# A two-layer block on one core: the down projections computed as seven products of halves instead of eight

## The reference

```python
D_FF = 2816; DEEPNORM_ALPHA = (2 * DEPTH) ** 0.25
def conv_ffn(x, w_up, conv_w, conv_b, w_down):
    up = x @ w_up                                  # 512 x 1024 by 1024 x 5632
    a, g = up[..., :D_FF], up[..., D_FF:]
    g = causal_dwconv(g, conv_w) + conv_b
    return (jax.nn.gelu(g) * a) @ w_down           # 512 x 2816 by 2816 x 1024
# in the layer:
x = layer_norm(alpha * x + conv_ffn(x, ...), ln_ffn_g[layer], ln_ffn_b[layer])
```

## Time and profile before

| | before |
|---|---|
| median of three runs | 1784.28 us |
| profiled execution, its own time | 1786.04 us |
| its span | 1784.2 us |
| PE busy | 1758.9 us (99% of the span) |
| DVE, ACT, POOL busy | 1027.2, 652.2, 99.5 us |
| granted TensorE clock | 0.998 mean |
| DMA | 189.67 MB, 106 GB/s |

### The profile page before, as it was taken

One profiled execution on the slowest core, in us unless ns is written; L12 is line 12 of the kernel. 1 busy time (PEld: TensorE's weight loads), 2 busy tenths in 40 slices (PEclk: granted clock), 3 DMA queues, 4 the chain that ended last, 5 costly groups with the idle time before them and its releaser, 6 DMA issues.

```text
span 1784.2 us, 27491 instructions
## 1 busy us (share of the span) xinstructions
PE 1758.9 (99%) x11571; PEld 1472.9 (83%) x11571; DVE 1027.2 (58%) x1480; ACT 652.2 (37%) x1013; POOL 99.5 (6%) x136
## 2 busy tenths in 40 slices
PE   8999999999999999999999999999999999999998
PEld 7888988988888889888998888888888767777766
DVE  5567267444445555454726755566556585566784
ACT  5232352323324333213235232232343553344552
POOL 3102002000000001000200200000001000011000
PEclk9999999999999999999999999999999999999999
DMA  9323312433333324333331264444431422112512
GB/s 302 111 94 113 113 49 77 147 95 102 98 95 107 94 83 128 109 95 117 108 107 60 89 195 153 142 154 130 138 94 36 151 60 73 38 38 63 176 36 83
DMA packets 146010, 189.67 MB, mean 106 GB/s; under 512 B 7800, under 2 KB 95092, under 8 KB 145120
## 3 DMA queue, kind: packets, MB, share of 16 engines
q1 hardware_dynamic: 140928, 172.59, 31.2%
q0 software_dynamic: 3488, 10.07, 1.8%
q10 hardware_dynamic: 1472, 5.26, 0.8%
HBM read 181.58 MB, written 6.30 MB: 105 GB/s over the span
## 4 chain that ended last, share of the span: by engine, by line
PE 93%; DVE 4%; issue 1%; ACT 1%; POOL 1%; DMA 0%; SPq 0%; DVEq 0%; ACTq 0%
PE ps L329 28%; PE ps L331 27%; PE ps L330 27%; PE ps L970 2%; PE ps L518 1%; PE ps L2222 1%; PE ps L2242 1%; PE ps L1628 1%; PE ps L2236 1%; PE ps L2256 0%; DVE LATE L2303 0%; PE ps L2359 0%; PE ps L982 0%; DVE WL L313 0%; PE ps L1652 0%
## 5 line engine op out<-in xcount | busy, mean ns | idle before, releaser
L313 DVE TENSOR_TENSOR WL<-RAW,WH 128x1024 fp32r<-128x1024 f32 x289 | 350.8, 1223 | 501.3 <-ACT WH L303 500.0
L329 PE MATMUL ps<-XH,WH 128*128 128x512 f32 (+1 forms) x1416 | 524.6, 371 | 3.4 <-DVE XL L1498 1.6
L303 ACT ACTIVATE WH<-RAW 128x1024 fp32r<-128x1024 f32 x289 | 303.5, 1058 | 597.5 <-PE ps L331 570.0
L331 PE MATMUL ps<-XH,WL 128*128 128x512 f32 (+1 forms) x1416 | 518.2, 366 | 0.0
L330 PE MATMUL ps<-XL,WH 128*128 128x512 f32 (+1 forms) x1416 | 517.9, 366 | 0.0
L329 PE MATMUL ps<-WH,XH 128*128 128x512 f32 x784 | 312.7, 399 | 2.4 <-DVE WL L313 1.1
L329 PEld LDWEIGHTS ps<-XH,WH 128*128 128x128 f32 x1416 | 267.5, 189 | 51.4 <-issue 6.1
L331 PE MATMUL ps<-WH,XL 128*128 128x512 f32 x784 | 305.8, 390 | 0.0
L330 PE MATMUL ps<-WL,XH 128*128 128x512 f32 x784 | 305.5, 390 | 0.0
L331 PEld LDWEIGHTS ps<-XH,WL 128*128 128x128 f32 x1416 | 267.4, 189 | 43.4
L330 PEld LDWEIGHTS ps<-XL,WH 128*128 128x128 f32 x1416 | 267.7, 189 | 40.9
(11 more groups left out here) (359 smaller groups left out, 1797.5 us busy)
## 6 DMA issues: line engine op xcount, KB each, us to landing
RAW<-ffn_w_up SPq DMA_DIRECT2D x176, 256.0 KB, 3.2
RAW<-ffn_w_down SPq DMA_DIRECT2D x44, 512.0 KB, 3.7
RAW<-w_in SPq DMA_DIRECT2D x33, 512.0 KB, 3.9
RAW<-xa_wkv SPq DMA_DIRECT2D x32, 512.0 KB, 3.8
RAW<-c_w_in SPq DMA_DIRECT2D x24, 512.0 KB, 3.8
LATE<-w_ada SPq DMA_DIRECT2D x24, 512.0 KB, 4.8
RAW<-xa_wq SPq DMA_DIRECT2D x16, 512.0 KB, 5.7
RAW<-xa_wo SPq DMA_DIRECT2D x16, 512.0 KB, 3.7
```

What stands on the lines that cost most here:

```text
L303: e.activation(halves_of(i)[0][:, :, 0:w], raw(i)[:, :, 0:w], ACT.Copy).then_inc(*w_hi.up(i))
L313: e.tensor_tensor(wl[:, :, 0:w], raw(i)[:, :, 0:w], wh[:, :, 0:w].bitcast(F), ALU.subtract).then_inc(*w_lo.up(i))
L329: e.matmul(o, lh, rh, start=start, stop=False)
L331: return e.matmul(o, ll, rh, start=False, stop=stop)
```

## The change

Both down projections are computed by Strassen's scheme in Winograd's form. The product is cut into halves: tokens 0 to 255 and 256 to 511, k rows 0 to 1407 and 1408 to 2815, output columns 0 to 511 and 512 to 1023. Seven products of halves take the place of eight. Each has 11 k tiles, two token tiles (u = 0, 1) and three matmuls of 512 columns: 66 matmuls. Their operands are sums:

- Weights: four sums t1 to t4 of quarter matrices (2.9 MB each) are made in memory by DMAs that POOL issues, a plain copy from memory to memory and then an accumulating one (`sums_pool`, six steps for each layer, spread over the stages before). Each copy and each accumulation is 2 DMAs, 16 DMAs for a layer. SP waits for them before it loads a chunk made of them.
- Tokens: four sums for each of 11 pairs of tiles of hT by four DVE operations of 256 columns (`token_sums`; nine times during the last five blocks of the up projection, twice in the down projection). One stays in hT, three go to memory (`token_out`) and two kinds come back (`token_in`) through a ring of three places, all issued by POOL.
- PE runs chunks of half the size of work: 40 chunks for a layer (22 that serve two products each, then 6 for each of the products c, d, e; the last of the 6 is half full), each used by 12 matmuls instead of 24. In the program of ACT and DVE a "step" s is one such chunk: at step s they split chunk s + 5 and the token items of `items_at(s)`.
- The results are combined by DVE in steps 20 to 29, then d closes rows 0 and 1 (steps 30 to 33), and e closes rows 2 and 3. In d and e the last four chunks are run for u = 0 first and then for u = 1.

```diff
+    def w_fast(l):
+
+        first["ffn", l] = len(chunks)
+        w = I["ffn_w_down"][l]
+        for name, k in FAST:
+            if name == "a":
+                chunks.append(([((0, 1), 512, w[128 * k:128 * k + 128, 0:512].unsqueeze(1)),
+                                ((1, 2), 512, d_sum[l][k][:, 2:3, :])], 512, ("t1", l, k)))
+            if name == "b":
+                chunks.append(([((0, 2), 512, d_sum[l][k][:, 0:2, :])], 512, ("t3", l, k)))
+            if name in "cd":
+                c = 512 * "cd".index(name)
+                chunks.append(([((0, pair(k)), 512, w[1408 + 256 * k:1408 + 256 * k + 128 * pair(k), c:c + 512].rearrange(
+                    "(k p) n -> p k n", p=P))], 512, None))
+            if name == "e":
+                v = d_sum[l][2 * k:2 * k + pair(k)]
+                chunks.append(([((0, pair(k)), 512, v[:, :, 3, :].rearrange("k p n -> p k n"))], 512, ("t4", l, 2 * k + pair(k) - 1)))
...
+            if chunks[i][2] is not None:
+                what, l, k = chunks[i][2]
+                for name in (("t2", "t3") if what == "t3" else (what,)):
+                    e.wait_ge(*sum_in[name][k // 6].at(l))
...
+    def token_sums(e, l, k):
+
+        pair_of, last = token_place(l)
...
+        e.wait_ge(*ffn_v.at(("h", l, 11 + k)))
+        e.tensor_tensor(s3, a11, a21, ALU.subtract).then_inc(*ffn_v.up())
+        e.wait_ge(*latest["V"])
+        e.tensor_tensor(a21, a21, a22, ALU.subtract).then_inc(*ffn_v.up(("s1", l, k)))
+        e.wait_ge(*latest["V"])
+        e.tensor_tensor(s2, a21, a11, ALU.subtract).then_inc(*ffn_v.up())
+        e.wait_ge(*latest["V"])
+        e.tensor_tensor(last, a12, s2, ALU.add).then_inc(*ffn_v.up(("s", l, k)))
...
+    def item_hi(e, l, n):
+
+        name, k = ITEMS[n]
+        if n < 2:
+            e.wait_ge(*(gemm.at(("kvv", 1, 3, 1)) if l else xa_pe.at(("pv", 0, 3, 1))))
+        elif name == "C":
+            for a in range(2 * k, 2 * k + pair(k)):
+                e.wait_ge(*x_lo.at(("item", l, ITEMS.index(("A", a)))))
+        elif RINGED.index(n) < 8:
+            e.wait_ge(*gemm.at((("up", l, 10), 3)))
+        else:
+            e.wait_ge(*gemm.at(("used", first["ffn", l] + item_last(RINGED[RINGED.index(n) - 8]))))
+        if name == "A":
+            e.wait_ge(*ffn_v.at(("s1", l, k)))
+        elif name in "BD":
+            i = LOADED.index((name, k))
+            e.wait_ge(*tok_in[i % 3].at((l, i)))
+        else:
+            e.wait_ge(*ffn_v.at(("h", l, 10 + 2 * k + pair(k))))
+        e.activation(item_view(n, item_home(l, n)[0]), item_from(n), ACT.Copy).then_inc(*x_hi.up(("item", l, n)))
+
+    def item_lo(e, l, n):
+
+        e.wait_ge(*x_hi.at(("item", l, n)))
+        hi, lo = item_home(l, n)
+        e.tensor_tensor(item_view(n, lo), item_from(n), item_view(n, hi).bitcast(F), ALU.subtract).then_inc(
...
+
+        def added(name, g, src):
+            e.wait_ge(*sum_in[name][g].at((l, "copy")))
+            e.dma_start(part(name, g), src, accum_op=ALU.add).then_inc(*sum_in[name][g].up(l))
+        for g in range(2):
+            if step == 0:
+                copied("t1", g, block(0, 1, g))
+                copied("t3", g, block(0, 1, g))
+            if step == 1:
+                added("t1", g, block(0, 0, g))
+                added("t3", g, block(1, 1, g))
+            if step == 2:
+                e.wait_ge(*sum_in["t3"][g].at(l))
+                copied("t2", g, part("t3", g))
+            if step == 3:
+                added("t2", g, block(0, 0, g))
+            if step == 4:
+                e.wait_ge(*sum_in["t2"][g].at(l))
+                copied("t4", g, part("t2", g))
+            if step == 5:
+                added("t4", g, block(1, 0, g))
...
+    def tokens_pool(e, l):
+        for k in range(9):
+            token_out(e, l, k)
+            if 2 < k < 6:
+                token_in(e, l, k - 3)
+
+    def down_pool(e, l):
+        for i in range(3, 17):
+            token_in(e, l, i)
+            if i == 6:
+                token_out(e, l, 9)
+            if i == 8:
+                token_out(e, l, 10)
...
+            e.wait_ge(*w_lo.at(i0 + s))
+            ready(s)
+            of = ((1, 0), (5, 256)) if name == "A" else ((6, 256), (7, 0))
+            for half, (p, at) in enumerate(of):
+                for u in range(2):
+                    key = ("down", l, p, u)
+                    if k == 0:
+                        ps.take(key)
+                        for w in ps.vacant(key):
+                            e.wait_ge(*w)
+                    r = product(key, s, at + 128 * u, i0 + s, half, k == 0, k == 10)
+                    names = [key] * (k == 10) + [("used", i0 + s)] * (half and u)
+                    if names:
+                        r.then_inc(*gemm.up(*names))
+            if k == 10:
+                ps.back(*[("down", l, p, u) for p, _ in of for u in range(2)])
+
+        def part(name, q, u):
+            i, m, key = i0 + FAST.index((name, q)), ITEMS.index((name.upper(), q)), ("down", l, {"c": 2, "d": 3, "e": 4}[name], u)
+            if u == 0:
+                e.wait_ge(*w_lo.at(i))
+                ready(m)
+            if q == 0:
+                ps.take(key)
+                for w in ps.vacant(key):
+                    e.wait_ge(*w)
+            for k in range(pair(q)):
+                at = 256 * u + 128 * k if name == "e" else 256 * k + 128 * u
+                r = product(key, m, at, i, k, (q, k) == (0, 0), q == 5)
+            names = [key] * (q == 5) + [("used", i)] * u
+            if names:
+                r.then_inc(*gemm.up(*names))
...
+                part("c", q, u)
+        ps.back(("down", l, 2, 0), ("down", l, 2, 1))
+        for name in "de":
+            for q in range(2):
+                for u in range(2):
+                    part(name, q, u)
+            for u in range(2):
+                for q in range(2, 6):
+                    part(name, q, u)
+                    if name == "e" and (u, q) in ((0, 5), (1, 3)):
+                        behind(u)
+        ps.back(*[("down", l, p, u) for p in (3, 4) for u in range(2)])
...
+    def items_at(s):
+
+        got = [s + 8] if s < 14 else []
+        got += [ITEMS.index(("C", q)) for q, at in enumerate((2, 6, 10, 13, 16, 18)) if at == s]
+        got += [ITEMS.index(("D", q)) for q, at in enumerate((14, 16, 17, 19, 22, 23)) if at == s]
+        return got + [ITEMS.index(("E", q)) for q, at in enumerate((24, 26, 28, 29, 30, 31)) if at == s]
...
+        def row(t):
+            u = t % 2
+            if t < 2:
+                e.wait_ge(*gemm.at(("down", l, 3, u)))
+                e.wait_ge(*ln_v.at((n, "x12", u)))
+                add(3, t, 1)
+                stats_of(t, 1)
+            else:
+                e.wait_ge(*gemm.at(("down", l, 4, u)))
+                e.wait_ge(*ln_v.at((n, "x21", u)))
+                add(4, t, 0)
+                stats_of(t, 0)
+            norm_g_dve(e, XR[:, t, :], n, t, 2, GB[:, 0:1024], gb_in.at(n))
...
+                if s == 20:
+                    e.wait_ge(*dn_a.at(("u", l, u)))
+                    scaled(u, 0, U[u]).then_inc(*ln_v.up((n, "x11", u)))
+                if s == 21:
+                    e.wait_ge(*gemm.at(("down", l, 6, u)))
+                    e.wait_ge(*ln_v.at((n, "x11", u)))
+                    e.tensor_tensor(U[u], U[u], ps.tile(("down", l, 6, u))[:, :], ALU.add).then_inc(
+                        *ps.empties(("down", l, 6, u), ln_v, (n, "sum", u)))
+                if s == 22:
+                    e.wait_ge(*ln_v.at((n, "sum", u)))
+                    e.wait_ge(*gemm.at(("down", l, 5, u)))
+                    e.tensor_tensor(Y[u], ps.tile(("down", l, 5, u))[:, :], U[u], ALU.subtract).then_inc(
+                        *ps.empties(("down", l, 5, u), ln_v, (n, "y", u)))
+                if s == 23:
+                    e.wait_ge(*ln_v.at((n, "y", u)))
+                    scaled(u, 1, Y[u]).then_inc(*ln_v.up((n, "x12", u)))
+                if s == 24:
+                    e.wait_ge(*gemm.at(("down", l, 7, u)))
+                    scaled(2 + u, 0, ps.tile(("down", l, 7, u))[:, :]).then_inc(*ln_v.up((n, "ax21", u)))
+                if s == 25:
+                    scaled(2 + u, 1, Y[u]).then_inc(*ln_v.up((n, "ax22", u)))
+                if s == 26:
+                    e.wait_ge(*ln_v.at((n, "ax22", u)))
+                    e.tensor_tensor(x(2 + u, 1), x(2 + u, 1), ps.tile(("down", l, 7, u))[:, :], ALU.subtract).then_inc(
+                        *ps.empties(("down", l, 7, u), ln_v, (n, "x22", u)))
+                if s == 27:
+                    e.wait_ge(*ln_v.at((n, "ax21", u)))
+                    e.tensor_tensor(x(2 + u, 0), x(2 + u, 0), U[u], ALU.add).then_inc(*ln_v.up((n, "x21", u)))
+                if s == 28:
+                    e.wait_ge(*gemm.at(("down", l, 2, u)))
+                    add(2, u, 0)
+                    stats_of(u, 0)
+                if s == 29:
+                    e.wait_ge(*ln_v.at((n, "x22", u)))
```

(32 more changed lines are left out.)

390 lines of the change are left out of this document (253 added, 137 removed).

## The result

| | before | after |
|---|---|---|
| median | 1784.13 us (4 runs, 1783.92 to 1784.6) | 1764.99 us (4 runs, 1762.02 to 1770.95) |
| ratio, 95% interval | | 0.9897 [0.9871, 0.9922] |
| profiled execution, its span | 1786.04, 1784.2 us | 1764.57, 1762.8 us |

The kernel is 1.0% faster. Forecast was 1760.3 us with a range of 1753.5 to 1774. The profiled execution came to 1764.57 where the sum said 1762.0.

What follows compares the result with a forecast made beforehand. PE, busy 99% of the span, was taken as the bound. Terms -29.9 -0.4 +4.8 +0.7 +0.8 = -24.0 us took the profiled 1786.0 to 1762.0, median 1760.3 us, range 1753.5 to 1774.

Steps and rivals of the forecast that it cites:

- PE's own work: Both down projections: 132 matmuls fewer at 0.2267 us each, 29.9 us off (about 28.5 by the skill's 518 cycles).
- Ordinary steps and the up projection's end: ACT and DVE keep up in ordinary down-projection steps, and token sums in the up projection's last five blocks cost nothing: 0.
- Start of the down projection: DVE's convolutions and item 7's token load at the down projection's start: 0 taken, bounds 0 and 3 us a layer.
- (c): Steps 20 to 33 of each down projection: PE waits for DVE's chunks 37 and 38, 2.4 us a layer, 4.8 in both.
- Chunk 42 behind the first layer: After the first layer's last down-projection matmul PE waits 0.7 us for this weight chunk from DVE; bounds 0 and 3.
- The second weight copy: End of the second layer: two weight copies instead of one between row 3's square and scaling, 0.8 us; bounds 0 and 1.1.
- The sums: Weight sums made in memory beside the weight loads: 0, bounds 0 and 3 us at each of four places.
- rival 3: Weight loads land late at the four bursts of weight sums, 1.5 to 3 us each: 1768 us; chance 0.12.
- the cover: Time by which weight loads may land late without a stall, read behind a norm as some 15 us.
- From the profiled execution to the median: Whole kernel: the median lies 1.76 us below the profiled execution, the same difference applied after the change.
- Rival 2: DVE bounds the down projections' last products: 8 us a layer instead of 2.4, 1.5 at the start; 1774.5 us; chance 0.17.

Runs made afterwards that it cites:

- the experiment: The changed kernel with one weight copy instead of two between row 3's square and its scaling, end of the second layer: 1764.07 us, ratio 0.9875.
- the late work: The changed kernel with six more statistics readings on DVE (4.1 us a layer) in steps 22 to 27 of each down projection: 1773.88 us, ratio 0.9933.

## Why the prediction held, and where it did not

- *PE's own work*, -29.9: right. 132 instructions fewer, 0.226 us apart. The spacing decides for 29.9 and against 28.5 (518 cycles); that PE's busy time fell by 28.7 does not speak for the latter, as other things changed in it too.
- *Ordinary steps and the up projection's end*, 0: right. No wait of PE between 560 and 640 us. DMA was put at 240 GB/s and is 240 and 253; DVE's busy share was put at 85% and is 89%.
- *Start of the down projection*, 0: right, no wait there.
- *(c), 2.4 us a layer*: right in the first layer (2.54) and in its place: two waits, for chunks 37 and 38, 1.3 and 1.1 forecast, 1.08 and 1.46 measured. In the second layer it is **mis-sized by 1.8 us** (4.24). The step that failed took both layers as alike. It followed DVE's queue, but not POOL's, in which `rms_pool(0)` stood before `norm_pool(1)`: the prediction said only that the norms stand behind the token DMAs. Of the 1.8 us, POOL's order is 0.9, and 0.6 is the chunk of down weights that landed late in the first profile; 0.3 stay open.
- *Chunk 42 behind the first layer*, 0.7: did not appear, as the waits in product e had already delayed PE. With these removed it came, at 1.2 us.
- *The second weight copy*, 0.8: in its place it is 0.9 us (from square to scaling 2.09 us before, 2.96 after). Of this 0.2 is left at the next stage's first product (12.44 us before, 12.61 after, from the bias product on), and 0.3 to 0.5 in the experiment. The 0.2 flatters it: in the trace of before the clock fell at 1387.1 us, and the transposes of row 3 began 0.9 us after their scaling had ended (1388.24 to 1389.15), behind slow ones; after, they began at once.
- *The sums*, 0: nearly right for the time, wrong in the landing (14.4 us where 7.5 was the most allowed; by turns between the queues rival 3 reckoned with twice a load's usual time, and it was four times, which decides). Rival 3 had the mechanism, at a much smaller price than its 8 us: 1.3 us in the first profile (0.55 near 380 us, 0.8 at the attention's start), 0.2 to 4.0 in others. The prediction read the cover only behind a norm. In the up projection it took the lead of five chunks as enough for DVE's token sums and did not ask whether the loads beside the sums of weights would use it up, as they did from 340 to 375 us.
- *From the profiled execution to the median*: I took off 1.76 us, since before's profile lay so much above its median. After's profile lies 0.4 us below its median. Of the 4.7 us between 1760.3 and 1764.99, 2.2 are this step, and 2.6 the sum: +1.8 and +0.1 in (c), +1.3 for the sums, -0.7 for chunk 42 and -0.6 for the copy make 1.9. Of the rest, two pieces have nothing to do with the change: +0.65 in the next stage's first products, where the 6.8 us of lower clock lay over more matmuls than in the trace of before, and -0.7 in the program's first 40 us. They cancel, and about 0.6 in the two down stretches stays unassigned. That the median came within 4.7 us owes something to such cancelling.
- *Rival 2* named the right engine. Its price, all of 43 - 35.4 us a layer, was too high, because the five chunks of lead pay for the most part. What is added on top is paid almost in full, as the chunk that landed late (0.51 us of DVE, 0.56 us of PE) and the first layer with the late work (3.9 of 4.1 us) showed.

What stays open is the spread. Executions of the changed kernel lie between 1762 and 1771 us, and slower ones have a lower mean clock (0.999 at 1762.02, 0.996 at 1770.95). The traces show two parts of it. One is the late loads beside the sums, 0.2 to 4.0 us. The other is the lower clock level, in stretches of 3.4 or 6.8 us: in eleven of the thirteen traces of the changed kernel and its variants behind the second layer's end, in three of eight behind PE's waits in product e of that layer (at 1341.9, 1347.2 and 1349.7 us), and in a few elsewhere (379.4, 1580.7 and 1584.6 us). But 0.003 of the mean clock is 5.3 us of 1763 (an estimate), not the 9 between the fastest and the slowest execution, so the clock alone does not make the spread. The slowest execution has no trace, and how the 9 us are made up stays open.

## What to carry to other kernels

When the busiest engine loses work, follow the queue of every engine that is fed by the freed time, POOL's too: a short instruction that waits for another engine delays all that stands behind it. An order of instructions is worth less than the stall it removes where the engine is full (6.2 us of waits gone, 3.2 gained); a stall that is taken away at one place comes back at the next, so move the work into an idle gap or take it off. And test the margin of a term that you put at zero: twice the traffic of the sums turned 20 us of gain into 14 us of loss. Look for such a term in every stage that runs beside the new traffic, not only in the one that is changed: the up projection at 340 to 375 us had no wait of PE before and had lost its whole lead after. And lay traces over each other matmul by matmul before a difference is called unassigned.

## What the runs showed of the hardware

- Accumulating and plain copies in memory fill the DMA engines (share 0.99 and 1.09, 0.37 without them): 512 KB loads beside them landed in 14.4 us in the median instead of 3.6, and 256 KB loads in 13.2 instead of 3.1, four times as long.
- An addition of 512 columns on POOL, two inputs in SBUF, beside DVE's: 1.77 us instead of 1.04, and DVE's operations at the same time lost 0.7 and 1.1 us. A POOL operation on 128 x 1 numbers took 1.41 us beside DVE's subtraction and 0.55 with DVE idle.
- After 4 us in which PE was busy for only 1.21 us, the granted clock fell to its lower level, and a series of 25 transposes took 1.6 us longer; with useless matmuls in the idle time it stayed up. It also stayed up once after 4 us with PE busy for 1.09 and nothing filled.
